# Scores of the dilated attention in three f16 passes, with GpSimd behind the rotary

## The reference

```python
h = x
h = h + hybrid_mixer(rms_norm(h, norm1_g), ...)            # gated linear attention + dilated attention
h = h + memory_cross_attention(rms_norm(h, norm2_g), mem, ...)
h = h + moe_ffn(rms_norm(h, norm3_g), ...)                 # top 4 of 32 experts, 12 MB of weights each
return rms_norm(h, final_norm_g)
```

## Time and profile before

| | |
|---|---|
| median of 3 runs | 1226.86 us |
| the profiled execution | 1226.35 us, its span 1224.6 us |
| TensorE busy | 1151.0 us (94%) |
| VectorE, ScalarE busy | 419.3 us, 262.1 us |
| GpSimd busy | 16.8 us |
| HBM read | 456.57 MB, 374 GB/s over the span |
| granted TensorE clock | 0.986 |

### The profile page before, as it was taken

How to read it: one execution, slowest core, us unless ns; L and a number is a source line. 1 busy time by engine, 2 the same in 40 slices (tenths; PEclk the granted TensorE clock), 3 DMA queues, 4 the chain that set the end, 5 groups by cost and what they waited for, 6 DMA issues and landing times.

```text
span 1224.6 us, 16091 instructions
## 1 busy us (share of the span) xinstructions
PE 1151.0 (94%) x6703; PEld 572.5 (47%) x6703; DVE 419.3 (34%) x822; ACT 262.1 (21%) x456; POOL 16.8 (1%) x40
## 2 busy tenths in 40 slices
PE   9999999999999999898989997998988899989896
PEld 7888989887433333233324332332332233224232
DVE  6789684775421221122122112221212122122112
ACT  5555465464400110010001000100100010001001
POOL 3000000000000000000000000000000000000000
PEclk9999999999999999999999999999999999999899
DMA  8765425976799999999999999999999999999996
GB/s 295 285 210 204 170 96 212 383 307 240 279 427 428 435 431 432 427 431 437 429 431 422 428 425 432 433 429 424 432 431 433 433 424 435 428 431 429 428 420 266
DMA packets 30410, 458.46 MB, mean 374 GB/s; under 512 B 3616, under 2 KB 3632, under 8 KB 6288
## 3 DMA queue, kind: packets, MB, share of 16 engines
q1 hardware_dynamic: 29088, 454.57, 88.9%
q0 software_dynamic: 832, 2.51, 0.6%
q10 hardware_dynamic: 432, 0.55, 0.1%
HBM read 456.57 MB, written 1.05 MB: 374 GB/s over the span
## 4 chain that ended last, share of the span: by engine, by line
PE 67%; DMA 26%; SPq 2%; ACT 2%; issue 1%; DVE 1%; POOL 0%; ACTq 0%; DVEq 0%
PE bank L2012 24%; DMA ring<-in_w_gate_up 19%; PE bank L2036 12%; DMA ring<-in_w_down 7%; PE bank L1574 5%; PE bank L1551 4%; PE sums L1667 3%; PE sums L1965 3%; PE sums L1551 3%; PE sums L1574 3%; SPq L467 2%; PE bank L1955 2%; PE bank L1667 2%; PE bank L2027 2%; PE sums L1607 1%
## 5 line engine op out<-in xcount | busy, mean ns | idle before, releaser
L2012 PE MATMUL bank<-ring,reg_a 128*64 128x512 f32 x2000 | 457.3, 609 | 36.2 <-DMA ring<-in_w_gate_up 35.5
L2012 PEld LDWEIGHTS bank<-ring,reg_a 128*64 128x64 f32 x2000 | 144.0, 140 | 315.6 <-issue 267.3
L2036 PE MATMUL bank<-ring,reg_ol 128*64 128x512 f32 x1024 | 227.2, 595 | 9.6 <-DMA ring<-in_w_down 8.4
L1468 DVE TENSOR_TENSOR masks<-bank,bT 128x256 f32<-128x256 f32 x64 | 27.2, 425 | 435.9 <-PE bank L2027 435.8
L2036 PEld LDWEIGHTS bank<-ring,reg_ol 128*64 128x64 f32 x1024 | 75.2, 137 | 139.9 <-issue 130.6
L663 ACT ACTIVATE reg_t<-bank 128x512 f32<-128x512 f32 x64 | 38.2, 597 | 425.5 <-PE bank L2012 230.3
L1013 DVE SCALAR_TENSOR_TENSOR ring<-ring 128x2048 f16<-128x2048 f32 x47 | 107.4, 2289 | 40.3 <-ACT ring L681 40.0
L968 ACT ACTIVATE masks<-masks 128x256 f32<-128x256 f32 x64 | 26.7, 417 | 335.1 <-DVE masks L1469 335.1
L681 ACT ACTIVATE ring<-ring 128x2048 f16<-128x2048 f32 x47 | 89.6, 1908 | 21.7 <-PE bank L1667 6.7
L1455 DVE COPY reg_t<-bank 128x512 f32<-128x512 f32 x32 | 22.1, 692 | 169.0 <-PE bank L2012 169.0
L1965 PE MATMUL sums<-reg_t,reg_g 64*128 64x512 f32 x256 | 69.8, 634 | 6.2 <-ACT reg_t L663 6.2
(11 more groups left out here) (329 smaller groups left out, 883.0 us busy)
## 6 DMA issues: line engine op xcount, KB each, us to landing
ring<-in_w_gate_up SPq DMA_DIRECT2D x42, 4096.0 KB, 29.9
ring<-in_w_down SPq DMA_DIRECT2D x21, 4096.0 KB, 30.0
ring<-in_w_gate_up SPq DMA_DIRECT2D x33, 2048.0 KB, 30.1
ring<-in_w_dense SPq DMA_DIRECT2D x47, 1024.0 KB, 4.9
ring<-in_w_down SPq DMA_DIRECT2D x16, 2048.0 KB, 29.7
ring<-in_w_gate_up SPq DMA_DIRECT2D x16, 1024.0 KB, 19.0
ring<-in_w_down SPq DMA_DIRECT2D x10, 1024.0 KB, 25.6
annex<-in_w_gate_up SPq DMA_DIRECT2D x4, 512.0 KB, 7.7
```

The source lines that it names most:

```text
L2012: ins = mm(pt[nh][col:col + 64, :], xg[:, c, j * SLOTS:(j + 1) * SLOTS], w[:, i * 512:(i + 1) * 512], start=(c == 0), stop=(c == C - 1))
L2036: ins = mm(pt[2][64 * nh:64 * nh + 64, :], actT[:, 4 * i + c, :], w[:, nh * 512:(nh + 1) * 512], start=(i == 0 and c == 0), stop=(i == 1 a ...
```

## The change

The rotated queries and keys are kept as two f16 parts instead of one f32 value, in the same space. VectorE only multiplies by cos and sin, into one of two `rot` buffers in turn, and frees the bank. GpSimd (new `rotated`) subtracts, adds and copies the f16 high part; VectorE (new `rotated_low`) takes the low part one rotary later. GpSimd does the units 0 and 1 ahead of its masks and the others behind them. `dil_scores` multiplies in three f16 passes, and TensorE waits for all low parts once before it. In the first norm VectorE squares and sums tile 0, scales the gains, then squares and sums tile 1. `gather(3)` moves from behind chunk 1 to behind chunk 3. The unit SPARE is loaded in two halves, the first already ahead of the half "xo1" (behind bank bd3). Semaphores of early loads are used again for the pieces of the last group.

```diff
@@ -178,12 +178,13 @@
 
         slot = [region(ring, s * WIDE, WIDE) for s in range(NSLOT)]
         at = FIRST_SLOT * WIDE
-        qr = region(ring, at, NG * 2, 2, T)
-        kr = region(ring, at + 3072, NG * 2, 2, T)
+        qr, kr = (region(ring, at + i * 3072, 3072).bitcast(F16)
+                  .rearrange("p (k g j t) -> p k g j t", k=2, g=NG * 2, j=2) for i in range(2))
         vd = region(ring, at + 6144, TT * NG * NH * DH).bitcast(F16).rearrange("p (k t n) -> p k t n", k=2, t=TT)
         kS = region(ring, at + 9216, 2, TT, NSUB, P)
         S = region(ring, at + 11264, 2, 9 * P)
-        rot = region(ring, at + 11264, 2, 2, T)
+        rot = [region(ring, at + 11264 + i * 1024, 2, 2, T) for i in range(2)]
+        turned = [region(ring, at + 14080 + i * 512, 2, T) for i in range(2)]
         PT = region(ring, at + 13568, 2 * NG * 3 * P).bitcast(F16).rearrange("p (h g k n) -> p h g k n", h=2, g=NG, k=2)
         B = region(ring, at + 13568, 2, T)
...
         AHEAD = HALF // 2
+        ROTATED = [(r, 2 * g + a) for r in (qr, kr) for g in range(NG) for a in range(2)]
+        NAMES = [f"{k}{g}{a}" for k in ("q_d", "k_d") for g in range(NG) for a in range(2)]
...
-        once = [spare_ld] + extra_ld
+        once = [(spare_ld, 32)] + [(done, 16) for done in extra_ld + ld_x + [ld_ahead, ld_vecs]]
         counted = [(v, i) for v, n in sorted(LAST_PIECES.items()) for i in range(n)]
-        piece_ld = {k: (once[i], 16) if i < len(once) else (sem(f"piece_ld{k[0]}_{k[1]}"), 0)
+        piece_ld = {k: once[i] if i < len(once) else (sem(f"piece_ld{k[0]}_{k[1]}"), 0)
...
+                if name == "xo0":
+                    take(sp, "bd3")
+                    held(SPARE, spare[:, 0:WIDE // 2], 0, WIDE // 2, spare_ld)
                 if u >= HALVES.index("gla1") and (u - HALVES.index("gla1")) % 2 == 0 and first[0] < NSLOT - EARLY:
                     first_unit()
             per = UPE * EG
             first_unit()
             take(sp, "xs3")
-            held(SPARE, spare, 0, WIDE, spare_ld)
+            held(SPARE, spare[:, WIDE // 2:], WIDE // 2, WIDE // 2, spare_ld)
...
@@ -634,10 +641,23 @@
             link(pool.memset(masks[:, 0:2, :], 0.0))
             pool.affine_select(out=masks[:, 0, :], in_=masks[:, 0, :], compare_op=ALU.is_ge, fill=NEG, base=0,
                                pattern=[[1, P]], channel_multiplier=-1).then_inc(masks_ready, 1)
+            def rotated(u):
+
+                r, i = ROTATED[u]
+                w, o = rot[u % 2], turned[u % 2]
+                emptied(pool, NAMES[u])
+                pool.tensor_tensor(o[:, 0, :], w[:, 0, 0, :], w[:, 1, 1, :], ALU.subtract)
+                link(pool.tensor_tensor(o[:, 1, :], w[:, 0, 1, :], w[:, 1, 0, :], ALU.add))
+                pool.tensor_copy(r[:, 0, i], o).then_inc(rot_high, 1)
+
+            rotated(0)
+            rotated(1)
             pool.wait_ge(mod_ready, 1)
             for m in (1, 3, 5):
                 pool.affine_select(out=masks[:, m, :], in_=masks[:, m, :], compare_op=ALU.is_ge, fill=NEG,
                                    base=0, pattern=[[-1, P]], channel_multiplier=1).then_inc(masks_ready, 1)
+            for u in range(2, len(ROTATED)):
+                rotated(u)
             root(2, 4)
...
-            for t in range(TT):
+            def x_squares(t):
+
                 dve.wait_ge(ld_x[t], 16)
                 link(dve.tensor_tensor_reduce(out=xn[:, t, D // 2:], in0=h[:, t, D // 2:], in1=h[:, t, D // 2:], scale=1.0,
                                               scalar=0.0, op0=ALU.mult, op1=ALU.add, accum_out=ssq[:, 0, t, 1:2]))
-            for t in range(TT):
                 dve.wait_ge(norm_ss, t + 1)
                 dve.scalar_tensor_tensor(st[:, t:t + 1], ssq[:, 0, t, 0:1], D * EPS, ssq[:, 0, t, 1:2], ALU.add, ALU.add)\
                     .then_inc(root_asked, 1)
-            squared[0] = TT
-            roots[0] += TT
+
+            x_squares(0)
             dve.wait_ge(ld_vecs, 16)
             dve.tensor_scalar(vT[:, 0:8], vT[:, 0:8], D ** 0.5, None, ALU.mult)
             dve.tensor_scalar(vT[:, 24:28], vT[:, 24:28], 0.5 / WS, None, ALU.mult)
             dve.tensor_scalar(vT[:, 28:44], vT[:, 28:44], 0.5, None, ALU.mult).then_inc(ahead_dve, 1)
+            x_squares(1)
+            squared[0] = TT
+            roots[0] += TT
             for t in range(TT):
                 dve.wait_ge(root_done, t + 1)
                 dve.tensor_scalar(xn[:, t, :], h[:, t, :], st[:, t:t + 1], None, ALU.mult).then_inc(norm_xn, 1)
...
-            def rotary(name, dst, before):
-                if before:
-                    emptied(dve, before)
+            lows = [0]
+
+            def rotated_low():
+
+                u = lows[0]
+                lows[0] += 1
+                r, i = ROTATED[u]
+                dve.wait_ge(rot_high, u + 1)
+                dve.tensor_tensor(r[:, 1, i], turned[u % 2], r[:, 0, i], ALU.subtract).then_inc(rot_low, 1)
+
+            def rotary(name, u):
                 cut_ahead(name)
                 b = take(dve, name)
                 ps = b[:].rearrange("p (a b) -> p a b", a=2)
-                dve.tensor_tensor(rot[:, 0], ps, mid(cs[:, 0, :], 2), ALU.mult)
-                link(dve.tensor_tensor(rot[:, 1], ps, mid(cs[:, 1, :], 2), ALU.mult))
-                dve.tensor_tensor(dst[:, 0, :], rot[:, 0, 0, :], rot[:, 1, 1, :], ALU.subtract)
-                dve.tensor_tensor(dst[:, 1, :], rot[:, 0, 1, :], rot[:, 1, 0, :], ALU.add)\
-                    .then_inc(free_bank(name), 1)
+                w = rot[u % 2]
+                dve.tensor_tensor(w[:, 0], ps, mid(cs[:, 0, :], 2), ALU.mult)
+                dve.tensor_tensor(w[:, 1], ps, mid(cs[:, 1, :], 2), ALU.mult).then_inc(free_bank(name), 1)
+                if u:
+                    rotated_low()
 
             dve.wait_ge(trig_out, 2)
             link(dve.tensor_scalar(cs, cs, 1 / WS, None, ALU.mult))
-            before = None
             for g in range(NG):
                 for a in range(2):
-                    rotary(f"q_d{g}{a}", qr[:, 2 * g + a], before)
-                    before = f"q_d{g}{a}"
+                    rotary(f"q_d{g}{a}", 2 * g + a)
...
-            def rotary_keys(g, before):
+            def rotary_keys(g):
                 for a in range(2):
-                    rotary(f"k_d{g}{a}", kr[:, 2 * g + a], before)
-                    before = f"k_d{g}{a}"
-                return before
-
-            before = rotary_keys(0, before)
-            before = rotary_keys(1, before)
+                    rotary(f"k_d{g}{a}", 2 * (NG + g) + a)
+
+            rotary_keys(0)
+            rotary_keys(1)
             dve.wait_ge(gla_exp, 1)
             emptied(dve, "q_g")
             emptied(dve, "q_g1")
@@ -1181,7 +1208,8 @@
                     ins = dve.tensor_tensor(kS[:, :, t, i, 0:n], kS[:, :, t, i, 0:n], kg[:, :, t * P:t * P + n],
                                             ALU.mult)
             ins.then_inc(gla_qk, 1)
-            rotary_keys(2, before)
+            rotary_keys(2)
+            rotated_low()
...
                         n = (t + 1) * P
                         for j in range(2):
-                            last = [mm(b[:, o:o + n], qr[hp, 2 * g + a, j, t * P:(t + 1) * P], kr[hp, 2 * g + a, j, 0:n],
-                                       start=(j == 0), stop=(j == 1)) for b, hp in heads]
+                            for k, (pq, pk) in enumerate(PASSES):
+                                last = [mm(b[:, o:o + n], qr[hp, pq, 2 * g + a, j, t * P:(t + 1) * P],
+                                           kr[hp, pk, 2 * g + a, j, 0:n], start=(j == 0 and k == 0),
+                                           stop=(j == 1 and k == 2)) for b, hp in heads]
...
+            pe.wait_ge(rot_low, len(ROTATED))
             dil_scores(0)
...
-                        if j == 0 and nh == 0 and c == 1:
-                            gather(2)
-                            gather(3)
+                        if j == 0 and nh == 0 and c in (1, 3):
+                            gather(2 + c // 2)
                     ins.then_inc(z.h_full, 1)
```

## The result

The changed kernel takes 1230.54 us (median of 8 runs, 1229.45 to 1231.39) against 1226.86 (8 runs, 1226.40 to 1227.50): ratio 1.0030, 95% interval 1.0021 to 1.0039. It is 3.7 us slower; 1225.9 was predicted, and the measured time lies above the range. The profiled execution took 1229.45 with a span of 1227.7 (before 1226.35 and 1224.6), so it is at the low end of its runs.

A forecast was written before the change was run, and what follows sets the result against it. Expert weight DMA bounds the end from 400 us, so the stream's start, set by TensorE's earlier chain, counts. Gains 0.3 + 0.6 + 0.5 less 0.4 make 1.0 us: 1225.9 us as a median, range 1224.1 to 1229.0.

The forecast's parts named there:

- First norm: Reordered first norm: tile 0 scaled from 7.15 instead of 7.87, gain limited by weights; worth 0.3 us, bounds 0.2 and 0.7.
- Scores: f16 dil_scores: nothing gained in the first stage, 0.6 us in the second; bounds 0 and 1.2.
- rival (2): In the f16 scores, heads don't run side by side: 1229.6 us, chance 0.05.
- Gathers: gather(3) behind chunk 3 shortens the DMA hole after the first two expert pieces: worth 0.5 us, bounds 0.3 and 0.9.
- Rotary: Rotary split between VectorE and GpSimd: 0.4 us of TensorE stall charged, bounds 0 and 4.
- No wait: VectorE's first low-part subtraction finds GpSimd's unit finished near 57.2, before VectorE gets there at 58.5.
- 1 to 2 us before the first place: VectorE's loss over three rotaries and mask steps before the cut from 67.43, which has 1.4 us of slack.
- 1 to 1.7 before the second: VectorE's further loss before the cut from 104.99, which has 1.35 us of slack.
- pauses of 4.3 us before three cuts: VectorE's three pauses between the two places of small slack, largest 2.05 us, counted as room to absorb delays.
- 5 us of work: When VectorE waits for GpSimd's last units, TensorE still has 5 us of work before needing the result.
- Rival (1): VectorE and GpSimd take turns, hurting once VectorE's cycle exceeds 5.24 us: 4.2 us of stall, 1229.7 us, chance 0.13.
- affine_select of the earlier trace: GpSimd operation at 11.17 beside a VectorE cut took 0.34 against 0.28 us: at most 0.06 of hindrance seen.

The follow-up runs named there:

- norm: Kernel before with only the new order of the first norm: 1226.26 us (ratio 0.9995).
- rest: Kernel before with only the new order of the first norm and gather(3) behind chunk 3: 1225.80 us (ratio 0.9991).
- rest5: The same kernel as rest, run once more in five rounds: 1226.24 us (ratio 0.9995).
- writes: Changed kernel with GpSimd's subtraction, addition and copy replaced by five memsets that read nothing from SBUF, rotated values zero: 1225.68 us (ratio 0.9988).
- third: As both, plus the cut of v_d10 put ahead of the last two low parts in the last key unit: 1226.60 us (ratio 0.9997).
- f32turns: Changed kernel with f32 scores and no high or low parts; GpSimd only subtracts and adds into the f32 operands: 1225.99 us (ratio 0.9991).
- anchor: Changed kernel with VectorE's negated anchors for ScalarE taken ahead of the last query half's cut, not behind its rotary: 1228.59 us (ratio 1.0013).
- both: Changed kernel with the moves of anchor and cut together: 1227.51 us (ratio 1.0005).
- vector16: f16 scores with nothing on GpSimd: VectorE subtracts, adds and takes low parts, ScalarE takes high parts, anchors early: 1229.39 us (ratio 1.0021).
- cut: Changed kernel with the cut for v_d00 ahead of the products of the gated attention, anchors left late: 1230.44 us (ratio 1.0030).
- f16only: Changed kernel with the first norm and gathers as before, so f16 scores with GpSimd's rotary alone: 1231.03 us (ratio 1.0034).
- acthigh: As third, but ScalarE takes the high parts and GpSimd only subtracts and adds: 1238.97 us (ratio 1.0097).

## Why the prediction was wrong

**What bounds the kernel** held, with one limit. The first expert's start and the end move together:

| kernel | first expert begins | last expert's final sums begin | between |
|---|---|---|---|
| before | 316.45 | 1215.45 | 899.0 |
| norm | 316.02 | 1214.93 | 898.9 |
| rest, rest5 | 315.99, 315.96 | 1214.39, 1214.27 | 898.4, 898.3 |
| writes | 315.08 | 1214.58 | 899.5 |
| third | 316.55 | 1214.78 | 898.2 |
| f32turns | 316.63 | 1215.16 | 898.5 |
| anchor | 317.60 | 1217.51 | 899.9 |
| both | 317.40 | 1217.73 | 900.3 |
| vector16 | 319.57 | 1218.20 | 898.6 |
| after | 319.92 | 1218.57 | 898.7 |
| cut | 320.83 | 1219.87 | 899.0 |
| f16only | 321.01 | 1220.65 | 899.6 |
| acthigh | 328.80 | 1227.79 | 899.0 |

The stage between varies by about 1 us either way from one execution to the next, which is as much as most terms of my sum.

**First norm, 0.3:** right in its mechanism; the size isn't settled. The scaling starts at 7.08 (7.15 predicted), the weights land and are taken at 9.26 (9.3 predicted), and TensorE is 0.47 earlier at 44 us (44.41 for 44.88). But in all twelve traces with the new order VectorE waits for that first weight half, which it takes between 9.08 and 9.86, and TensorE reaches this place 35.15 to 35.26 us later, between 44.24 and 45.07. In f32turns, where the weights came last, it is 0.19 later than before. F16only, with the old order, waits for them too (9.55, then 44.70). The mean of the twelve is 44.54, 0.25 under the mean of the two with the old order. So the weights bound the gain, as predicted, and how large it looks in one pair of traces is largely luck of when they landed. (In the prediction's sum, 14.50 less 1.31 is 13.19 and not 13.24; nothing hangs on it.)

**Scores, 0.6:** right. Heads run side by side, which settles rival (2). The first stage gives nothing, its wait is 1.21 (1.3 predicted, 0.15 before); in the second TensorE goes from 4.19 late to 3.47 late, 0.72. Rest and writes, which differ by the scores, stand 0.91 us apart at the first expert, 0.19 of it from the start; their medians differ by 0.1. So the gain is in the trace, and within the error of the times.

**Gathers, 0.5:** the hole closes as said, but its worth isn't settled. The stage between takes 899.0, 898.9 and 899.6 us in the three traces with the old order (before, norm, f16only) (mean 899.2), and 898.2 to 900.3 in the eleven with the new one (mean 899.0).

**Rotary, 0.4: this is the step that failed.** It measured 4.67. Its parts, as the prediction put them:
- The price of one operation was right, and the price of a unit too low. I took 0.65 for one GpSimd operation and one delay of a cut per unit, against 0.3 saved. Measured are 0.72 for GpSimd's addition, 0.61 for the copy and 0.52 per turn; but where VectorE doesn't pause, as in anchor from 83 to 98 us, each cut pays one and every second low part another, so a unit pays 0.9 (4.91 against the 4.00 of writes).
- "No wait" for the first subtraction was wrong: GpSimd's first operation was held by the cut (2.85 us from 54.73), and VectorE stood 0.78 before its first low part at 58.97.
- "1 to 2 us before the first place" was right: VectorE's cuts go from 1.25 us early to 0.57 late, 1.8. That cut also takes 0.52 longer, so it ends 1.09 late while TensorE is 0.47 early: 1.6 against a slack of 1.4, and TensorE's stall there is 0.27. "1 to 1.7 before the second" was wrong: the cut there is 4.56 late.
- What was wrong is what I set against it afterwards: pauses of 4.3 us before three cuts, the largest 2.05, counted as slack. They are waits for ScalarE, and ScalarE had been waiting for VectorE's anchors (2.46 us before L681). When VectorE is late, the anchors are late, ScalarE is late by 3.34, and the pause does not shrink but moves: VectorE still waits 1.98 at 85.77, 0.99 at 90.84 and 0.54 at 100.90, 3.5 of the 4.3. The real slack in that ring was ScalarE's, and it was not in my rows. Moving one small instruction (anchor) showed it: 2 us back with all turns in place.
- The products of the gated attention, with both inputs in SBUF, I left out of the turns: the first three meet GpSimd, 1.5 us more at the place of least slack.
- `rot_high` was a real wait at the end: VectorE stood 0.78 at 117.8 and 1.29 at 120.3 behind GpSimd's last units. I took TensorE to have 5 us of work by then; it had less, and the 0.93 at 125.6 is that. Third removed it by order.

**Rival (1)** gave 4.2 us of stall and 1229.7, the nearest of my cases, with a chance of 0.13. Its fact was right, its mechanism only half: nearly all of GpSimd's unit is covered, VectorE's cycle is 4.9 as a mean, below TensorE's 5.24, the point from which I said it would decide. The loss comes below that point, at lumps of work, and through ScalarE. The affine_select of the earlier trace rows that I held against the turns could not speak: it lies in front of the low parts, whose second input is in PSUM, and touches only the end of a cut. The Trainium skill (SBUF — State Buffer, "Who interferes with whom") says that a VectorE instruction with two SBUF inputs contends with a GpSimd instruction that reads SBUF and not with one that only writes; the rows here agree for such instructions: cuts and low parts grow only beside GpSimd's reads, and beside the memsets of writes they keep 2.28 or 2.29 and 0.68 or 0.69.

## What to carry to other kernels

A pause of an engine is slack only if the engine that it waits for doesn't wait for it in turn: follow each pause that you count on one step further back. Before work goes to GpSimd, list the inputs of what VectorE does beside it. Where a VectorE instruction with two SBUF inputs and a GpSimd instruction that reads SBUF meet, the one that comes second waits for the rest of the other: behind a cut GpSimd's 0.7 us became 2.7 to 2.8 and VectorE lost nothing (f32turns); where GpSimd was already waiting as VectorE went from its low part to its cut, VectorE lost 0.52. So one such VectorE instruction a unit was nearly free here, and two in a row were not. And when an engine's cycle comes near that of the engine it feeds (4.91 of 5.24 here, 4.32 before), the loss comes at the lumps (masks, a block of products), not in the steady part. Three moves of order, each taking what another engine waits for ahead of a long instruction, brought back 3.9 us with every turn in place (third); taking the copies and low parts away did as well (f32turns, 1225.99), and giving the high parts to ScalarE on top of the three moves lost 12.4 (acthigh).

## What the runs showed of the hardware

**The turns also reach instructions with one SBUF input**: the anchors, one input of 16 columns, take 0.69 us instead of 0.17 (83.10), and the first mask step 0.63 instead of 0.22, both with GpSimd reading. Beside GpSimd's memsets the same anchors take 0.39 (writes, 77.69), so for them writing is not free of cost either.

**TensorE's clock fell behind the longest stall.** In f16only and in cut TensorE had a wait of 2.69 and 2.63 us before 112, and then ran at a granted clock well under full. Windows of f16only, TensorE, clock, DMA share, GB/s:

```profile
108.00:112.00 4.00, 1.57 (x15) 1.00 0.00 0
112.00:116.00 4.00, 3.74 (x20) 0.58 0.72 238
116.00:120.00 4.00, 4.00 (x38) 1.00 0.77 264
```

0.58 over these 4 us is mostly the lower level, 1.2 GHz. The 96 matmuls take 12.31 us instead of 10.64; the wait of 0.9 that follows elsewhere is covered by that, so 0.7 us are lost. In the profiled execution of the changed kernel the same stall of 2.68 was followed by 10.64 at full clock. That execution is the lowest of eight, its median 1.1 above; some of the others may have had the lower clock, which no trace shows. In acthigh a wait of 2.52 us was followed by 96 matmuls in 12.04 us and a clock of 0.64 over 96 to 100 us, and one of 2.80 by 0.62 over 120 to 124. After waits of 2.17 there and of 1.76 and 1.92 us (vector16) the clock stayed at full.
